# A ring of five split weight blocks in the projection loop of a hybrid decoder step

## The reference, cut to what matters

```python
h = rmsnorm(x, g_mix)
proj = h @ w_in                 # (288, 1024) @ (1024, 10272)
# lru_in, lru_gate, z, xbc, dt_raw, gate_a, gate_b are slices of proj
u   = causal_dwconv(lru_in, ...)           # 4 taps
y_a = rg_lru(u, ...) * gelu(lru_gate)
xbc = silu(causal_dwconv(xbc, ...))        # x, B and C of the SSD branch
y   = ssd_chunked(x, dt, A, B, C, s0)      # 8 groups, state 128
y_b = grouped_rmsnorm((y + D * x) * silu(z))
merged = sigmoid(gate_a) * (y_a @ w_br_lru) + sigmoid(gate_b) * (y_b @ w_br_ssd)
```

## Time and profile before

| | us |
|---|---|
| median of three runs | 1065.55 |
| lowest, highest | 1062.95, 1066.67 |
| the profiled execution's own time | 1067.93 |
| its span | 1066.1 |
| TensorE matmuls busy in the span | 961.1 (90%) |
| VectorE busy | 563.2 (53%) |
| ScalarE busy | 400.5 (38%) |
| TensorE waiting for VectorE's low halves, all passes and the prologue | 30.8 in 10 waits |

### The profile page before, as it was taken

How to read it: one execution, slowest core, us unless ns; L and a number is a source line. 1 busy time by engine, 2 the same in 40 slices (tenths; PEclk the granted TensorE clock), 3 DMA queues, 4 the chain that set the end, 5 groups by cost and what they waited for, 6 DMA issues and landing times.

```text
span 1066.1 us, 16675 instructions
## 1 busy us (share of the span) xinstructions
PE 961.1 (90%) x5389; PEld 707.8 (66%) x5389; DVE 563.2 (53%) x1069; ACT 400.5 (38%) x679; POOL 166.4 (16%) x214
## 2 busy tenths in 40 slices
PE   5598899898998889989897999998999999999986
PEld 3487777777777777778684999776444444444465
DVE  2685665757657576575765654244324243243434
ACT  3455362564625646255464432135011111111232
POOL 0045133251332513325131000002000000000000
PEclk9788787998879988798896999989999999999998
DMA  7172262632626326262172751492799999999401
GB/s 190 40 171 81 63 184 58 181 85 64 183 58 182 84 65 182 57 182 80 46 219 73 207 160 39 137 390 76 268 386 389 385 384 393 389 371 392 133 1 45
DMA packets 208601, 188.52 MB, mean 177 GB/s; under 512 B 8000, under 2 KB 166392, under 8 KB 208568
## 3 DMA queue, kind: packets, MB, share of 16 engines
q1 hardware_dynamic: 207352, 187.12, 54.8%
q10 hardware_dynamic: 1216, 0.98, 0.3%
HBM read 176.88 MB, written 11.21 MB: 176 GB/s over the span
## 4 chain that ended last, share of the span: by engine, by line
PE 72%; DVE 10%; ACT 10%; issue 6%; DMA 1%; DVEq 1%; ACTq 0%; SPq 0%
PE bank L1703 11%; PE bank L1406 6%; PE bank L1731 5%; PE bank L1408 5%; PE bank L1407 5%; PE bank L1659 5%; PE bank L1567 4%; PE bank L1482 4%; PE bank L1666 4%; PE bank L1473 3%; PE bank L1596 3%; PE bank L1751 2%; ACT whi L699 2%; PE bank L1571 2%; DVE wlo L969 2%
## 5 line engine op out<-in xcount | busy, mean ns | idle before, releaser
L1406 PE MATMUL bank<-h_hi,whi 128*128 128x288 f32 x640 | 211.5, 330 | 30.8 <-DVE wlo L969 30.8
L1407 PE MATMUL bank<-h_lo,whi 128*128 128x288 f32 x640 | 203.3, 318 | 0.0
L1408 PE MATMUL bank<-h_hi,wlo 128*128 128x288 f32 x640 | 202.2, 316 | 0.0
L1406 PEld LDWEIGHTS bank<-h_hi,whi 128*128 128x128 f32 x640 | 134.8, 211 | 59.0 <-DVE wlo L969 36.4
L699 ACT ACTIVATE whi<-wb 128x1024 fp32r<-128x1024 f32 x82 | 86.8, 1059 | 133.8 <-PE bank L1408 123.9
L1407 PEld LDWEIGHTS bank<-h_lo,whi 128*128 128x128 f32 x640 | 135.0, 211 | 0.4
L1408 PEld LDWEIGHTS bank<-h_hi,wlo 128*128 128x128 f32 x640 | 134.5, 210 | 0.0
L1303 DVE TENSOR_TENSOR xT<-xT,bank 128x288 f32<-128x288 f32 x128 | 49.5, 448 | 152.3 <-PE bank L1666 152.3
L969 DVE TENSOR_TENSOR wlo<-wb,whi 128x1024 fp32r<-128x1024 f32 x82 | 104.6, 1276 | 38.0 <-ACT whi L699 31.1
L897 ACT ACTIVATE Gs<-bank 128x512 f32<-128x512 f32 x16 | 9.6, 597 | 144.5 <-PE bank L1703 144.5
L1567 PE MATMUL bank<-br_hi,whi 128*128 128x288 f32 x192 | 52.9, 302 | 8.3 <-ACT br_hi L824 6.9
(11 more groups left out here) (348 smaller groups left out, 1566.2 us busy)
## 6 DMA issues: line engine op xcount, KB each, us to landing
wb<-in_w SPq DMA_DIRECT2D x80, 1024.0 KB, 8.7
wb<-in_w_in SPq DMA_DIRECT2D x80, 512.0 KB, 4.0
wb3a<-in_w SPq DMA_DIRECT2D x16, 1024.0 KB, 8.7
arena<-in_state_ssd SPq DMA_DIRECT2D x16, 512.0 KB, 6.1
out_new_ssd_s<-arena SPq DMA_DIRECT2D x16, 512.0 KB, 5.8
wb<-in_w_br_ssd SPq DMA_DIRECT2D x16, 512.0 KB, 3.9
wb<-in_w_br_lru SPq DMA_DIRECT2D x8, 512.0 KB, 4.2
wb<-in_w_out SPq DMA_DIRECT2D x8, 512.0 KB, 3.9
```

The lines of the kernel that those rows point to most:

```text
L1406: mm(bP[i % 2][:, 0:T], hi, h_hi[:, k, :], start=(k == 0), stop=False)
L1407: mm(bP[i % 2][:, 0:T], hi, h_lo[:, k, :], start=False, stop=False)
L1408: ins = mm(bP[i % 2][:, 0:T], lo, h_hi[:, k, :], start=False, stop=(k == KC - 1))
```

## The change

The ring gets five entries. The low half of a block is written over the weight itself, in the slot of `wb` (named `wbR` where it is seen as fp32r). The high halves go round five buffers: the two of `whi`, the two of `wlo`, and the first 1024 columns of `hT`, which the projection does not use (`hTR`). Splits are made three blocks ahead instead of two: `large` and `small` stand at the places where they stood, each for the block one later; one more split stands in the prologue, ahead of the chain on dt. A slot of `wb` is free for the next load only when the multiplications of its block are done, so SyncE waits for `projected` instead of `w_small`. In the last pass the splits of the first two blocks of the branch stage keep to `whi` and `wlo`, as that stage expects.

The diff, cut to its core:

```diff
+        over_wb = ExitStack()
+        wb = over_wb.enter_context(nc.sbuf_tensor("wb", [P, 6, KC, P], F32))
+        over_wb.close()
+        wbR = ctx.enter_context(nc.sbuf_tensor("wbR", [P, 6, KC, P], F32R))
...
+        hi5 = [whi[0][:], whi[1][:], wlo[0][:], wlo[1][:], hTR[:].rearrange("p a b -> p (a b)")[:, 0:D]]
...
                 if s >= 5:
-                    sp_.wait_ge(w_small.sem, w_small.at(0, s - 4))
+                    sp_.wait_ge(projected.sem, projected.at(0, s - 4))
...
-                    sp_.wait_ge(w_small.sem, w_small.at(g, s - 4))
+                    sp_.wait_ge(projected.sem, projected.at(g, s - 4))
...
-            def large(g, b):
+            def large(g, b, last=False):
                 act.wait_ge(landed[b % 10 % 5], g * 32 + 16 * (1 + b // 5))
-                act_f(whi[b % 2][:], wflat(b % 10 % 5), ACT.Copy).then_inc(w_large.sem, 1)
+                dst = whi[b - 10][:] if last and b >= 10 else hi5[b % 5]
+                act_f(dst, wflat(b % 5), ACT.Copy).then_inc(w_large.sem, 1)
             large(0, 0)
             large(0, 1)
+            large(0, 2)
...
                 act.wait_ge(projected.sem, projected.at(g, i + 1))
-                large(g, i + 2)
+                large(g, i + 3, last)
...
-            def small(g, b):
-                s = b % 10 % 5
+            def small(g, b, last=False):
                 dve.wait_ge(w_large.sem, w_large.at(g, b + 1))
-                v.tensor_tensor(wlo[b % 2][:], wflat(s), whi[b % 2][:].bitcast(F32), ALU.subtract).then_inc(w_small.sem, 1)
+                hi, lo = hi5[b % 5], wbR[:, b % 5].rearrange("p a b -> p (a b)")
+                if last and b >= 10:
+                    hi, lo = whi[b - 10][:], wlo[b - 10][:]
+                v.tensor_tensor(lo, wflat(b % 5), hi.bitcast(F32), ALU.subtract).then_inc(w_small.sem, 1)
             small(0, 0)
             small(0, 1)
+            small(0, 2)
...
                 conv(g, 1, C_SW, 32, C_SB, 2 * g + 1)
-                small(g, 4)
+                small(g, 5, last)
                 conv(g, 2, C_SW, 32, C_SB, g + 16)
-                small(g, 5)
+                small(g, 6, last)
...
                     conv(g, 0, C_SW, 32, C_SB, 2 * g + 2, n=1)
-                    small(g, 13)
+                    small(g, 14)
...
-                    hi, lo = (t[i % 2][:, k * P:(k + 1) * P] for t in (whi, wlo))
+                    hi, lo = hi5[i % 5][:, k * P:(k + 1) * P], wbR[:, i % 5, k, :]
```

More of the change, by code:

```diff
@@ L172, in sbe @@
             return moe.enter_context(nc.sbuf_tensor(name, shape, dt))
-        wb = sb("wb", [P, 6, KC, P])
+        over_wb = ExitStack()
+        wb = over_wb.enter_context(nc.sbuf_tensor("wb", [P, 6, KC, P], F32))
+        over_wb.close()
+        wbR = ctx.enter_context(nc.sbuf_tensor("wbR", [P, 6, KC, P], F32R))
         wr = sb("wr", [P, KC, 20])
@@ L178, in build @@
         xT = sb("xT", [P, KC, T])
-        hT = sb("hT", [P, KC, T])
+        over_hT = ExitStack()
+        hT = over_hT.enter_context(nc.sbuf_tensor("hT", [P, KC, T], F32))
+        over_hT.close()
+        hTR = ctx.enter_context(nc.sbuf_tensor("hTR", [P, KC, T], F32R))
         ya = sb("ya", [P, KC, T])
@@ L515, in last_step @@
                 if s < 5:
-                    sp_.wait_ge(w_small.sem, w_small.at(G, s - 4))
+                    sp_.wait_ge(projected.sem, projected.at(G, s - 4))
             branch(0, 0, last_step)
@@ L720, in new_tokens, with evac @@
                 return v[:, SMP:PAD].rearrange("p (b r) -> p b r", r=7)[:, :, r0:r0 + NT]
-            def evac(g, i):
+            def evac(g, i, last=False):
                 act.wait_ge(projected.sem, projected.at(g, i + 1))
-                large(g, i + 2)
+                large(g, i + 3, last)
                 n = i % 10
@@ L745, in raw @@
                     act.wait_ge(projected.sem, projected.at(g, i + 1))
-                    large(g, i + 2)
+                    if not last or i + 3 < 12:
+                        large(g, i + 3, last)
                     ch.tell(act_f(dst, bP[i % 2][:, 0:T], ACT.Copy), proj_free, i + 1)
@@ L755, in group @@
                 silu(0)
-                evac(g, 2)
+                evac(g, 2, last)
                 silu(1)
-                evac(g, 3)
+                evac(g, 3, last)
                 silu(2)
-                evac(g, 4)
+                evac(g, 4, last)
                 silu(3)
@@ L763, in group @@
                     act.wait_ge(projected.sem, projected.at(g, 6 + j))
-                    large(g, 7 + j)
+                    large(g, 8 + j, last)
                     if j == 0:
@@ L1039, in conv @@
                                                    op0=ALU.mult, op1=ALU.add), conv_done, i + 1 + 5 * n)
-            small(0, 2)
+            small(0, 3)
             conv(0, 0, C_SW, 32, C_SB, 0)
-            small(0, 3)
+            small(0, 4)
             def group(g, last):
@@ L1073, in group @@
                 conv(g, 1, C_SW, 32, C_SB, 2 * g + 1)
-                small(g, 4)
+                small(g, 5, last)
                 conv(g, 2, C_SW, 32, C_SB, g + 16)
-                small(g, 5)
+                small(g, 6, last)
                 conv(g, 3, C_SW, 32, C_SB, g + 24)
-                small(g, 6)
+                small(g, 7, last)
                 conv(g, 4, C_LW, 8, C_LB, g)
-                small(g, 7)
+                small(g, 8, last)
                 tokens(0)
                 diff(0)
-                small(g, 8)
+                small(g, 9, last)
                 tokens(1)
@@ L1091, in group @@
                 weights(1)
-                small(g, 9)
+                small(g, 10, last)
                 tokens(2)
@@ L1095, in group @@
                 weights(2)
-                small(g, 10)
+                small(g, 11, last)
                 dve.wait_ge(Y_ready.sem, Y_ready.at(g, 2))
@@ L1111, in group @@
                     ch(ins) if j == 0 else ch.tell(ins, CU_free, 4)
-                small(g, 11)
+                if not last:
+                    small(g, 12)
                 dve.wait_ge(m_ready.sem, m_ready.at(g, 1))
@@ L1140, in group @@
                 if not last:
-                    small(g, 12)
+                    small(g, 13)
                 new_states(1)
```

## The result

The change made the kernel slower: 1077.63 us, median of four runs (1076.33 to 1079.55), against 1064.91 us for the kernel before, median of four runs (1062.95 to 1066.67). The ratio is 1.0121, with a 95% interval of 1.0095 to 1.0148. The forecast was 1066.

The account below looks back on a forecast made before the run. TensorE's 3.7 us waits for VectorE's low half ahead of block 4 were taken as the stall; -6.3 - 0.4 + 1.0 = -5.7 us, +6.3 for the clock, gave +0.6: 1066 us, range 1062 to 1069, for 8 in 10 1059 to 1072.

Parts of the forecast that it names:

- The waits for the split go, and a new one of 2.5 us comes ahead of C times B: Passes 1 to 6: TensorE's 3.7 us wait ahead of block 4 goes; 2.5 us idle ahead of line 1492 comes.
- The gain of 1.05 us a pass: Passes 1 to 6: C times B starts 1.05 us earlier, held by VectorE's convolutions; -6.3 us in six passes.
- the third rival: The whole stall ahead of block 4 and its slow block go, 31 us: 1034; chance 0.04.
- The third split in the prologue, +1.0: Prologue and pass 0: one more split of 1.18 us ahead of dt's chain, unhidden; pass 0 loses 1.0 us.
- Loads hidden, the split in place at the same cost: Later weight loads stay hidden by 1.5 us at least; VectorE's in-place split again takes 1.22 us, at most 1.35.
- falls in four or five of the six passes: Block 6, behind the new idle ahead of C times B: clock falls cost 1.4 us each, +6.3 us in all.
- The bound of 3.65 us: Upper bound per pass for a clock fall: 1.4 us on block 6 plus 2.25 if the small matmuls are doubled too.
- The second rival: Clock falls in every pass, block 6 paying on the path: 1071, or 1077 at 2.5 us a fall; chance 0.24.
- Whose slow block was harmless to all but itself: Kernel before: the slow block 4 behind the old stall, 4.76 us long, was said to delay nothing else.

Follow-up runs that it names:

- the second fill alone: Changed kernel with 16 unused matmuls only in the idle time ahead of line 1527 (xdte times btok), none ahead of C times B: 1066.46 us, ratio 1.0024.
- the order alone: Kernel before, without the ring, with block 6 multiplied ahead of C times B, the transposes and the rows: 1051.78 us, ratio 0.9861.
- both together: Changed kernel (ring, splits three blocks ahead) with block 6 multiplied ahead of C times B, the transposes and the rows: 1032.17 us, ratio 0.9685.

## Why the prediction was wrong, step by step

**The waits for the split go, and a new one of 2.5 us comes ahead of C times B: right.** It is 2.38 us, released by the SiLU.

**The gain of 1.05 us a pass: right in size.** The first column of the table gives 19.22 - 18.19 = 1.03 us. Its bound was the one named, VectorE's convolutions. In pass 2 they start here:

```profile
195.24 0.44 DVE L1040 TENSOR_SCALAR cv<-pad,par 128x312 f32<-128x312 f32 x1 [0.98 <-ACT xbc L746]
...
197.88 1.23 DVE L981 TENSOR_TENSOR wbR<-wb,whi 128x1024 fp32r<-128x1024 f32 x1
```

From 195.24 to C times B at 206.14 it is 10.90 us; 10.9 was forecast. The rule of the Trainium skill on repeated gaps, which stood behind the third rival (Perfetto Trace Analysis, Identifying Performance Opportunities), is borne out by half: one more block of buffering ended that gap, and the next releasers put it back: 22.2 us of waits for the split went in six passes, and 23.1 us of waits for the bank and the SiLU came. Pass 7 gained 0.43 us, with 0.4 forecast.

**The third split in the prologue, +1.0: right in size, though the rows at first seem to deny it.** C times B of pass 0 starts 0.30 us later:

```profile
43.97 0.47 PE L1431 MATMUL bank<-cst,arena 32*128 32x32 f32 x3 [4.28 <-DVE arena L1003]
...
69.75 0.48 PE L1506 MATMUL bank<-xbc 128*128 128x128 f32 x2 [2.04 <-ACT xbc L746]
```

The chain of dt ended 0.22 us later only (43.97 against 43.75). But in this execution the first two splits start at 31.79 us, with 32.72 before. From the start of the first split to line 1431 it is 12.18 us, where it was 11.03: the third split costs 1.15 us. The earlier start is no part of the change. In the runs with the same prologue the splits start anywhere from 31.68 to 33.68 us; in the one with the second fill alone it is 32.87, and there C times B of pass 0 starts at 70.58, 1.13 us later than before. Why this start differs isn't shown. (The idle time in brackets is 4.28 us, where it was 1.58, because blocks 0 and 1 ahead of it also took 6.61 us where they took 8.17.)

**Loads hidden, the split in place at the same cost: right.** No wait of TensorE, VectorE or ScalarE between 119 and 535 us is released by a landing. The split takes 1.23 us, 1.22 before; the ring with splits two ahead has the time of the kernel before.

**The clock, "1.4 us, the value measured on a block, and falls in four or five of the six passes": this is the step that failed.** The mechanism was named, and its place. It was put at 4.5 x 1.4 = 6.3 us. The second column, over all eight passes, adds up to 66.55 us after and 8 x 5.55 = 44.4 before: 22.1 us, or 2.8 us a fall and eight falls. Three things were taken too small:

- The price of one fall was read from block 4 of the kernel before: one dense block, at a lower clock for 4.76 us. Here the low clock began at the small matmuls and lasted through most of block 6, so the rows lost 0.95 us (2.07 against 1.12) and block 6 2.13 (5.58 against 3.45) in pass 2. The bound of 3.65 us had held both; the value was taken from the row that is nearest in shape, not from what stands in the place.
- The count was six passes. Passes 0 and 7 get the idle time as well (2.04 and 1.59 us) and fell too. They have little or no gain to set against it.
- A fall was left out in a quarter of the passes (4.5 of 6), since pass 7 of the kernel before had 2.58 us of idle without one. With block 6 first in the kernel before, the same 2.6 us in pass 7 were followed by a block of 6.13 us. One row without a fall was no evidence for safety.

Against the 22.1 us stand 4.8 us that came back in the last column (over eight passes 233.1 and 228.3), where the small matmuls ahead of block 9 (2.7 us) and block 9 itself (1.7 us) had less of the lower level. The whole: 22.1 for the falls, -6.2 and -0.4 gained in passes 1 to 6 and in pass 7, -4.8, +0.3 in pass 0, +0.2 for the third column and +0.4 behind the loop, together 11.6 us, the difference of the spans. The second rival had the mechanism, and with "2.5 a fall" its far end of 1077; it was put at 1071 and the range ended at 1072. That its far end meets the measured time is in part luck: it counted 7 x 2.5 = 17.5 us of falls, where 22.1 were lost and 4.8, which it did not foresee, came back.

**"Whose slow block was harmless to all but itself": half true.** Filling that stall showed that it cost 0.9 us a pass. A fall on block 4 was partly hidden behind VectorE's list, while a fall on the rows and block 6 comes through whole: the stretch behind it, from line 1516 to 1527, is as long as before (12.21 and 12.18 us).

## What to carry to other kernels

Where a stall is moved, not removed, ask what the clock's fall behind it will lie on: behind block 4 a part of it was covered, behind C times B it was on the path, and the fall cost 2.8 us a pass instead of 0.9, though the idle time ahead of it was shorter (2.4 us instead of 3.7). Price such a fall by the work that stands in that place, small matmuls included, and count it in every pass that gets the idle time. Before a deeper ring is added, look for work that the engine can do in the time it frees: the ring with splits three blocks ahead lost 1.2%, the order alone gained 1.4%, both together 3.1%.

## What the runs showed of the hardware

- Unused matmuls made this kernel faster: 32 of them in each pass, some 4.6 us of TensorE's time, took 31.8 us off the changed kernel's time.
- The mean clock over the span doesn't price it well: it is 0.910 in the kernel before and 0.905 after, so the low level held for 2 x 0.090 x 1066.1 = 192 us and 2 x 0.095 x 1077.7 = 205 us. The Trainium skill (TensorE: Matmul & The Clock Gate, section Terms) takes the penalty as about the throttled time by the share of the clock that is lost; by it the estimate here is half of 13 us, 6.5 us. The rows show 10.0 us of longer busy time. Part of the difference is that low time had lain under an idle engine: in passes 0 to 7 the traces' clock records put 130.7 us of low level over TensorE's matmuls before and 147.6 after, and half of that rise is 8.5 us. The rest isn't explained.
- After the same idle time of 1.24 us the clock fell in three passes and held in three others; the cause of this isn't settled.
